# First tiles after a normalisation ordered by kind of product, with small unread products before the transposes, and three groups of transfers moved

## The reference, cut to what matters

```python
for l in range(DEPTH):                      # DEPTH = 2
    proj = x @ w_in[l]                      # x: 256 x 1024, w_in: 1024 x 2560
    q, k, v, a, g = split(proj)
    attn = moba_attention(rope(q), rope(k), v)          # 8 heads of 64, causal
    conv = conformer_conv(a, g, ...)        # a * sigmoid(g), 31 taps, LayerNorm, silu
    mixed = concatenate([attn, conv]) @ w_out[l]        # 1024 x 1024
    x = layer_norm(DEEPNORM_ALPHA * x + mixed, ln1_g[l], ln1_b[l])
    ffn = peer_ffn(x, peer_wq[l], peer_keys[l], peer_u[l], peer_v[l])
    x = layer_norm(DEEPNORM_ALPHA * x + ffn, ln2_g[l], ln2_b[l])
```

## Time and profile before

| | us |
|---|---|
| median of three runs | 1935.8 (1935.02 to 1936.09) |
| the profiled execution | 1935.18 |
| its span | 1933.4 |
| TensorE busy | 1901.8 (98%) |
| VectorE busy | 1478.7 (76%) |
| ScalarE busy | 976.0 (50%) |
| GpSimd busy | 359.1 (19%) |
| share of the 16 DMA engines, main queue | 49.6% |

### The profile page before, as it was taken

The page is one execution under the profiler, slowest core; times in us unless marked ns, Lnnn a source line. Parts: engine busy times, 40 slices in busy tenths (PEclk is TensorE's granted clock), DMA queues, the critical chain, the costliest instruction groups (busy, mean ns, idle before and its releaser), DMA issues.

```text
span 1933.4 us, 38435 instructions
## 1 busy us (share of the span) xinstructions
PE 1901.8 (98%) x12952; PEld 1628.5 (84%) x12952; DVE 1478.7 (76%) x2598; ACT 976.0 (50%) x1631; POOL 359.1 (19%) x266
## 2 busy tenths in 40 slices
PE   8999999999999999999999999999999999999998
PEld 8779998888887888888787799988888878888886
DVE  7978998788888888544488789987888888884444
ACT  6455456555554444444465554565555544444444
POOL 0000000000004444444400000000000044444543
PEclk9999999999999999999999999999999999999999
DMA  6244555554544454755552445565444444547553
GB/s 222 98 144 160 175 197 190 169 168 160 170 159 166 157 171 162 238 185 186 161 169 96 164 144 180 190 196 173 162 163 163 164 163 163 165 161 243 189 186 119
DMA packets 90489, 328.33 MB, mean 170 GB/s; under 512 B 10048, under 2 KB 10560, under 8 KB 90176
## 3 DMA queue, kind: packets, MB, share of 16 engines
q1 hardware_dynamic: 87264, 316.71, 49.6%
q10 hardware_dynamic: 3168, 10.89, 1.7%
HBM read 324.41 MB, written 3.15 MB: 169 GB/s over the span
## 4 chain that ended last, share of the span: by engine, by line
PE 88%; DVE 7%; ACT 2%; issue 2%; DMA 1%; POOL 0%; DVEq 0%; SPq 0%; ACTq 0%; POOLq 0%
PE bank L1464 19%; PE bank L1232 14%; PE bank L1234 13%; PE bank L1233 13%; PE bank L1463 9%; PE bank L1483 5%; PE bank L1219 4%; PE bank L1220 4%; PE bank L1221 4%; DVE conv_acc L796 1%; PE bank L1466 1%; DVE lo L708 1%; PE bank L1306 1%; DVE top_index_u L943 1%; DVE top_values L936 1%
## 5 line engine op out<-in xcount | busy, mean ns | idle before, releaser
L708 DVE TENSOR_TENSOR lo<-raw,hi 128x1024 fp32r<-128x1024 f32 x600 | 764.6, 1276 | 237.1 <-ACT hi L409 235.9
L409 ACT ACTIVATE hi<-raw 128x1024 fp32r<-128x1024 f32 x600 | 633.4, 1057 | 458.0 <-PE bank L1234 442.2
L387 POOL TENSOR_TENSOR w_split<-h,w_split 128x256 fp32r<-128x256 f32 x256 | 357.7, 1398 | 1558.7 <-ACT w_split L644 1162.7
L1464 PE MATMUL bank<-xt,hi 128*128 128x512 f32 x1600 | 562.4, 397 | 0.0
L1232 PE MATMUL bank<-hi,w_split 128*128 128x512 f32 x1024 | 409.5, 400 | 0.7 <-POOL w_split L387 0.7
L1234 PE MATMUL bank<-hi,w_split 128*128 128x512 f32 x1024 | 404.5, 395 | 0.0
L1233 PE MATMUL bank<-lo,w_split 128*128 128x512 f32 x1024 | 404.1, 395 | 0.0
L1463 PE MATMUL bank<-xt,lo 128*128 128x256 f32 x1400 | 394.2, 282 | 0.0
L1464 PEld LDWEIGHTS bank<-xt,hi 128*128 128x128 f32 x1600 | 291.9, 188 | 51.8
L1463 PEld LDWEIGHTS bank<-xt,lo 128*128 128x128 f32 x1400 | 263.0, 188 | 9.0
L1219 PE MATMUL bank<-xt,hi 128*128 128x256 f32 x832 | 239.8, 288 | 4.3 <-DVE xt L721 3.8
(11 more groups left out here) (176 smaller groups left out, 1775.2 us busy)
## 6 DMA issues: line engine op xcount, KB each, us to landing
raw<-in_stream SPq DMA_DIRECT2D x600, 512.0 KB, 3.4
ln_g<-in_ln_p ACTq DMA_DIRECT2D x4, 512.0 KB, 8.2
ln_b<-in_ln_p ACTq DMA_DIRECT2D x4, 512.0 KB, 10.7
keys_sb<-in_keys_t ACTq DMA_DIRECT2D x2, 1024.0 KB, 5.2
x_kept<-x ACTq DMA_DIRECT2D x4, 512.0 KB, 4.2
x<-x_kept ACTq DMA_DIRECT2D x4, 512.0 KB, 7.8
x<-in_x SPq DMA_DIRECT2D x2, 512.0 KB, 4.9
result<-x SPq DMA_DIRECT2D x4, 256.0 KB, 2.0
```

The lines of the kernel that those rows point to most:

```text
L387: nc.gpsimd.tensor_tensor(ws[:, j, 1, :], h[:, ds(i * (RING * SEQ) + j * SEQ, SEQ)], ws[:, j, 0, :].bitcast(f32), ALU.subtract).then_inc(* ...
L409: nc.scalar.activation(hi[:, j, :], raw[:, j, :], ACT.Copy).then_inc(*hi_done.one)
L708: vec.tensor_tensor(lo[:, j, :], raw[:, j, :], hi[:, j, :].bitcast(f32), ALU.subtract).then_inc(*lo_done[j].one)
L1464: last = mm(dst[:, :], w_hi, both, start=k == 0, stop=k == KC - 1)
```

## The change

1. Where x is new, the first tiles go by kind of product (`first_by_x`): for each of them all 8 products high by high, which wait for `hi_done` and for `xt_hi`; then for each its 8 products with the low part of x (waiting for `xt_lo`), its wait for `lo_done` and the 8 with its own low part. It is done for two tiles at the three normalisations, and for one at the start. The sums are the same up to the order of addition.
2. Before the transposes TensorE does small products whose results nobody reads (`keep_clock`): a bf16 identity by a 128 x 128 bf16 table into the places that the transposes then write. 44 of them before the transposes of the second half at each normalisation; at the start 20 before the first half and 4 before the second. TensorE's wait for the table (`masks_made`) moves to the beginning.
3. At the second normalisation of the first layer ScalarE makes the high parts of the next layer's first two tiles between its two roots, and not after them.
4. The loads of `rope_sb`, `ln1_g` and `ln1_b` move from ahead of the AG tiles to behind them. The write of x to memory moves from before the first query tile to after the sixth (`KEEP_X = 5`).

```diff
+AT_START, AT_NORM = (20, 4), (0, 44)
+KEEP_X = 5
...
-                head(0, AG0)
+                if layer == 0:
+                    head(0, AG0)
                 x_heads(0)
-                for n in range(AG0 + 1, AG0 + HI_LEAD):
+                for n in range(AG0 + (2 if layer else 1), AG0 + HI_LEAD):
                     head(0, n)
...
+                    if n == WQ0 + KEEP_X:
+                        act.wait_ge(*x1_ready(layer, 2 * TT))
+                        for t in range(TT):
+                            act.dma_start(x1_dram[t * P:(t + 1) * P, :], x[:, t, :])\
+                               .then_inc(*x1_kept.one)
...
                 root(1, 0)
+                if layer + 1 < DEPTH:
+                    head(0, TILES + AG0)
+                    head(0, TILES + AG0 + 1)
                 root(1, 1)
...
+            pe.wait_ge(*masks_made(0, 2))
             for layer in range(DEPTH):
+                def keep_clock(count, t):
+
+                    for n in range(count):
+                        c, k = n % 4, n // 4 % 2
+                        mm(ring_banks[c][:, k * SEQ + t * P:k * SEQ + (t + 1) * P],
+                           ident_b[:, :], tri[:, :], start=True, stop=True)
+
-                def transpose_x(ready, before):
+                def transpose_x(ready, before, clock_products):
 
                     for t in range(TT):
+                        keep_clock(clock_products[t], t)
                         for c in range(4):
...
+                def first_by_x(n0, dsts, before):
+
+                    for n, dst in enumerate(dsts, n0):
+                        pe.wait_ge(*hi_done(layer, n + 1))
+                        for k in range(KC):
+                            if n == n0 and k % 2 == 0:
+                                pe.wait_ge(*xt_hi(layer, before + k // 2 + 1))
+                            mm(dst, weight(0, n % RING, k), xt[:, k, 0, :], start=k == 0,
+                               stop=False)
+                    for n, dst in enumerate(dsts, n0):
+                        for k in range(KC):
+                            if n == n0 and k % 2 == 0:
+                                pe.wait_ge(*xt_lo(layer, before + k // 2 + 1))
+                            mm(dst, weight(0, n % RING, k), xt[:, k, 1, :], start=False,
+                               stop=False)
+                        pe.wait_ge(*lo_done[n % RING](layer, n // RING + 1))
+                        for k in range(KC):
+                            last = mm(dst, weight(1, n % RING, k), xt[:, k, 0, :], start=False,
+                                      stop=k == KC - 1)
+                        last.then_inc(*tile_used.one)
...
-                transpose_x(x_ready, 2 * TT)
+                transpose_x(x_ready, 2 * TT, AT_NORM if layer else AT_START)
...
+                early = 2 if layer else 1
+                first_by_x(AG0, [ag_banks[0][e][:, 0:SEQ] for e in range(early)], 0)
+                for n in range(AG0 + early, QKV0):
...
-                transpose_x(x1_ready, 0)
-                for n in range(WQ0, U0):
+                transpose_x(x1_ready, 0, AT_NORM)
+                first_by_x(WQ0, [acc_banks[e][:, 0:SEQ] for e in range(2)], 4)
+                for n in range(WQ0 + 2, U0):
```

More of the change, by code:

```diff
@@ L439, in _ @@
                    .then_inc(*conv_in.one)
[L440 to L444, removed]
                 def qk_transposed(c):
@@ L469, in _ @@
                           .then_inc(*diags_made.one)
+                act.dma_start(rope_sb[:, :, :, :], rope).then_inc(*params_in.one)
+                act.dma_start(ln1_g[:, :], ln_p[ds(layer * 4, 1), :].to_broadcast([P, D]))\
+                   .then_inc(*params_in.one)
+                act.dma_start(ln1_b[:, :], ln_p[ds(layer * 4 + 1, 1), :].to_broadcast([P, D]))\
+                   .then_inc(*params_in.one)
                 def conv_from_ps(c):
@@ L556, in _ @@
                 head(0, WQ0 + 2)
-                act.wait_ge(*x1_ready(layer, 2 * TT))
-                for t in range(TT):
-                    act.dma_start(x1_dram[t * P:(t + 1) * P, :], x[:, t, :]).then_inc(*x1_kept.one)
                 def score_group(c):
@@ L1209, in transpose_x, with weight, tile_by_x @@
                                 last.then_inc(*xt_ps.one)
-                def tile_by_x(slot, dst, xt_before=None):
+                def weight(part, slot, k):
+                    return (hi, lo)[part][:, slot, k * P:(k + 1) * P]
+                def tile_by_x(slot, dst):
                     for k in range(KC):
[L1216 to L1221, removed]
-                    last.then_inc(*tile_used.one)
+                        mm(dst, weight(0, slot, k), xt[:, k, 0, :], start=k == 0, stop=False)
+                        mm(dst, weight(0, slot, k), xt[:, k, 1, :], start=False, stop=False)
+                        last = mm(dst, weight(1, slot, k), xt[:, k, 0, :], start=False,
+                                  stop=k == KC - 1)
+                    last.then_inc(*tile_used.one)
@@ L1285, in qk_transposed @@
                     last.then_inc(*qk_ps.one)
[L1287 to L1296, removed]
+                early = 2 if layer else 1
+                first_by_x(AG0, [ag_banks[0][e][:, 0:SEQ] for e in range(early)], 0)
+                for n in range(AG0 + early, QKV0):
+                    pe.wait_ge(*lo_done[n % RING](layer, n // RING + 1))
+                    tile_by_x(n % RING, ag_banks[(n - AG0) // 2][(n - AG0) % 2][:, 0:SEQ])
                 conv_work = ([(2, tap, diag2, PE_SHARE) for tap in range(PE_SHARE)]
@@ L1397, in _ @@
                 pe.wait_ge(*qk_done(layer, 4))
-                pe.wait_ge(*masks_made(0, 2))
                 scores(0)
@@ L1440, in _ @@
                         pe.wait_ge(*qp_done(layer, n - WQ0 - 3))
-                    tile_by_x(n % RING, acc_banks[(n - WQ0) % 4][:, 0:SEQ],
-                              xt_before=4 if n == WQ0 else None)
+                    tile_by_x(n % RING, acc_banks[(n - WQ0) % 4][:, 0:SEQ])
                     if n > WQ0 and (n - WQ0) % TOP_GROUPS == 0:
```

## The result

The changed kernel took 1925.88 us as the median of four runs (1923.17 to 1928.24). The four runs of the kernel before were 1935.02, 1935.80, 1936.09 and a new one of 1939.59. The ratio to the kernel before, run beside it, was 0.9929 with an interval of 0.9904 to 0.9954; it is 1925.88 / 1939.59, so it rests on that new run alone. So the absolute time is 0.7 us from the forecast of 1926.6, and the change is larger than forecast: 10.1 us by these medians, 13.7 by the ratio, against 9.2. The absolute time lies in my range of 1923.5 to 1931.4.

The account below looks back on a forecast made before the run. TensorE, 88% of the chain, bounds the kernel through standstills and the slow clock behind them. Gains 1.99 + 3.36 + 2.0 + 1.55 = 8.9 us took 1935.18 to 1926.3, stated as 1926.6 for the median; range 1923.5 to 1931.4.

Parts of the forecast that it names:

- The order of products: First normalisation: first product waits only for ScalarE's high part, wait for x's low parts goes; third tile starts 1.99 us earlier.
- The "7.1" among its signs: Sign in the profile after: third tile 7.1 us after the second half's first transposes (135.79 to 143.34), where it was 9.5.
- The small products: Before x at each normalisation: 44 at 0.059 us take 2.6 us, hidden in 2.9 us; gains assume the upper clock level.
- The border and the second layer: Same reordering at the layer border, 3.36 us as the slow stretch was longer there, and in the second layer, 2.0 us.
- The start: At the start: second tile at 12.5 against 13.35, 0.85 us, plus 0.7 us from the diagonals' wait; together 1.55 us.
- The moved transfers: Parameter loads and x write: at nothing themselves; moving the parameters removes the start's later wait for diagonals, 0.7 us with restart.
- what is late next: At the start, after the diagonals: VectorE's taps come next, but gain the same 2 us of ScalarE's wait.
- The rival at 1931.2: Clock falls anyway: slow stretches at normalisations stay, gains 0.8, 0.9, 0.8, with the start 4.0 in all; chance 0.12.
- A run differs from the next by 1 us: Basis of the range, with each attention's slow stretch costing about 1.7 us: 3 us downward and somewhat upward.
- the first rival: Clock falls anyway at normalisations, if small products and transposes don't act like steady products; 1931.2 us, chance 0.12.
- The dear small products: Rival at all three normalisations: 44 overrun 2.9 us; 1932.7 at 0.11 us each (chance 0.06), slower from 0.134 (0.03).
- VectorE's stage: Rival: VectorE's top-16 searches behind the query tiles bound there, losing the two gains at query tiles (4.0); 1930.6, chance 0.05.

## Why the prediction was right and wrong

**The order of products** was right in mechanism, and its place came out at 1.80 us for 1.99. Of that 0.6 us is the order itself (the run with the old one), the rest the clock. The first product waits for the high part alone, the wait for the low part is gone, and the third tile starts 7.7 us after the transposes. The forecast's own sum gives 143.34 - 135.79 = 7.55. The "7.1" among its signs was a slip of subtraction.

**The small products** fit as costed (0.056 us against 0.059) and hid. What I made of them was wrong, as my expectation for the run without them shows: I took them for what keeps the clock up and asked for 4.9 us; taking them away cost 0.9, so the new order alone does nearly all of it. With neither there is no gain that ten runs show (1936.7 against 1936.4). The gain seems to belong to the smaller standstill, whichever edit makes it small.

**The border and the second layer** came out at 3.22 and 1.89 for 3.36 and 2.0. In the border, 0.7 us depend on the early high parts, which the forecast had at nothing because it did not ask which tile's high part the 8 products of the second tile wait for.

**The start** gave 1.28 for 1.55. The second tile began at 12.98 and not at 12.5: the low parts of tiles start at 11.56, 0.41 us later than before (11.15), where I had put the four small products at 0.15. That is 0.37 us gained for 0.85. **The moved transfers** were put at the other 0.7; the stretch on which they act gained 0.91 (23.63 us from the second tile to the first tap product before, 22.72 after); with them undone the changed kernel loses 2.2. The step that was incomplete is the question of what is late next: I answered it for the first layer and not for the second, where a wait for diagonals of 1.0 us would have stood. Since the loads were moved in both layers, the sum was not hurt by it.

**Slips in the sum.** 1926.3 and 0.6 make 1926.9, not 1926.6, so the forecast change of 9.2 us is 0.3 above the gain of 8.9 that was worked out. The rival at 1931.2 was not given the 0.6 that the others have.

**The range failed at its low end**, by the ratio (1922.1) and not by the absolute time. The step that failed is "A run differs from the next by 1 us, and the slow stretch in each layer's attention ... may come or go", which I drew from three runs between 1935.02 and 1936.09. The runs showed 10 us in its place: the kernel before has runs from 1933.6 to 1943.3 with a median of 1936.4, the changed kernel from 1923.2 to 1930.4. The one run that the ratio rests on, 1939.59, is 3.2 above that median; against the median the change is 10.5 us, which on a before of 1935.8 is 1925.3, inside the range. The three runs I had were close to each other by chance, and the profiled execution was among the better ones: its mean granted clock, 0.994, is the highest that the 47 runs have. So that the absolute time came within 0.7 us of the forecast is in part luck: the before that I started from was low, and the clock's share too small.

The mean granted clock of a run falls short of 1 by half of the share of the span that was spent at 0.50, so it tells the loss without any step in between: 0.9924 as the mean of the 47 runs before, 0.9978 of the eight after. (1 - 0.9924) x 1935 = 14.7 us were lost to the lower level, (1 - 0.9978) x 1925 = 4.2 us are now. The difference, 10.5, happens to be as large as the whole measured change of the medians (1936.4 - 1925.9 = 10.5). That product counts slow time during waits and behind the last product as lost too, so that it is an upper bound for the clock's share. Part of the change can't be the clock's: three times 0.6 us for the order, by the run with the old one, and most of the 1.3 at the start. That leaves the clock some 7 to 8 us, an estimate from these numbers. My sum gave it about 4.9 of its 8.9, since it priced the falls of one execution.

**The rivals.** The clock did not fall behind the normalisations in any profile with both edits, so the first rival fell. Its condition, that small products and transposes don't do what steady products do, can be tested at the start. There the windows read 1.00 throughout, so the rise is read from the pace. In the run without small products the transposes start 0.213 us apart from 5.6 to 9.16, twice the 0.109 us of those at 132.01 in the kernel before; the second fp32 product starts at 9.59, and the next one 0.12 us behind it. So the rise came at 9.6, when TensorE had done 16 transposes since 5.6 and ordinary products only since 9.23:

```profile
5.62 3.96 PE L1222 MATMUL bank<-ident,x 128*128 128x128 f32 x16 [5.62 <-DVEq L708]
9.23 1.73 PE L1248 MATMUL bank<-xt,hi 128*128 128x256 f32 x8
```

The Trainium skill (TensorE: Matmul & The Clock Gate, "Part 4: PE-mode transpose") says that transposes don't count as busy for this. This trace disagrees, by the 0.36 us of ordinary products that stood before the rise.

The dear small products fell by their price. VectorE's stage moved with TensorE: the 7.0 us gained up to the second layer's query tiles were still there at the end (7.0). What stays open: the new order alone on the kernel before, without the moved transfers and early high parts, wasn't tried; nor was any standstill made longer on purpose to see at what length the clock falls; and why a fall in the attention lasts 3 us in one run and 10 in the next isn't settled by these runs.

## What to carry to other kernels

Where an engine with a clock that falls has a standstill, look for the granted clock behind it as well as for the wait itself, and price both; edits that shorten the same standstill replace each other, so undo them singly and together before saying which one works. A profile shows one execution: compare the mean granted clock of many runs before taking its falls for the typical ones. Small unread products are a cheap filler where an engine waits anyway (0.056 us each here), as long as they end before what it waits for; in the one run with 22, those did as well as 44. And look at how many runs a ratio rests on: here it was one, and it alone put the result outside the range.

## What the runs showed of the hardware that I had not expected

The same program spreads over 10 us (1933.6 to 1943.3) from one run to the next, and the time goes with TensorE's mean granted clock: the four runs with 0.990 took 1939.8 to 1943.3, the nine with 0.994 took 1933.6 to 1937.1. Closing two standstills of 1.9 us in the attention with small products brought the spread of eight runs from 7.2 to 1.2 us. A run of bf16 products of 128 columns goes at 0.056 us each at the upper level; at the start 20 of them stood for 5.72 - 3.64 = 2.1 us, 0.104 each, the pace of the lower level. Small products and transposes alone were followed by a rise, too: with the early high parts taken back, the transposes at the start go from 0.214 to 0.109 us apart at 6.3 us, before any ordinary product:

```profile
5.72 1.31 PE L1218 MATMUL bank<-ident,x 128*128 128x128 f32 x8
```
